# Turning attention probabilities in two 64-row halves of TensorE

## The chip, the core and the metric

The kernel runs on one core of a Trainium2 chip. The metric is the device time of one execution in microseconds (us), as the median of several runs. TensorE (PE in the rows) multiplies; its weight loads are shown as a row of their own, PEld. VectorE is DVE, ScalarE is ACT, GpSimd is POOL, SyncE is SP. Results of TensorE land in PSUM, which this kernel uses as eight banks of 512 float32 columns on 128 partitions.

## The reference

A decoder trunk of two layers on 512 positions of width 1024. Each layer runs a SwiGLU block, a mixer, a second SwiGLU block and a gated embedding. The mixer adds three kinds of heads. What matters here is the attention in it: 6 query heads in 2 key groups (sparse attention) and 4 differential heads.

```python
s_s = jnp.einsum('bqgrd,bgqkd->bgrqk', qblk, k_sel) * scale + bias
p_s = jax.nn.softmax(jnp.where((dist >= 0)[:, :, None], s_s, NEG), axis=-1)
o_s = jnp.einsum('bgrqk,bgqkd->bqgrd', p_s, v_sel)
...
s_w = jnp.einsum('bqgrd,bkgd->bgrqk', qblk, k_win) * scale + bias_w
p_w = jax.nn.softmax(jnp.where(valid_w, s_w, NEG), axis=-1)
o_w = jnp.einsum('bgrqk,bkgd->bqgrd', p_w, v_win)
...
a = p[:, :, 0] - lam * p[:, :, 1]
return jnp.einsum('bhqk,bkhd->bqhd', a, v)
```

## The kernel before

All matrices of weights stream through three slots: SP loads a chunk, ACT makes its high half (`weights_hi`, L983), DVE or POOL the low half (`weights_lo`, L1477 and L500), and TensorE does three products for each tile (L525 to L527). This part fills most of the time.

The attention works on ten **maps** for each layer, `u` = 0 to 9. Maps 0 to 5 are the sparse ones: `u // 2` is the head within a key group and `u % 2` says selected or window keys. Each holds both key groups, g = 0 and 1. Maps 6 to 9 are the differential heads. A map's probabilities lie in SBUF with the queries on the partitions, in four row blocks `i`, and for each block the key blocks `j` up to `i`: ten blocks of 128 x 128 for each g. To multiply them with the values, the keys must be on the partitions, so every block is turned: `transposes(u)` (L827) is a TensorE transpose with the block as the loaded weights and the identity as the moving operand. It writes PSUM, in three parts: part 0 has the 4 blocks of key block 0, part 1 the 3 of key block 1, part 2 the 3 of key blocks 2 and 3.

The turned blocks are copied to `probsT` in SBUF by ACT (`turned`, L1325) and by DVE (`evacuate`, L1897): ACT takes (g, part) = (0,0), (1,0), (0,2), DVE takes (0,1), (1,1), (1,2). Then `values(u)` (L847) multiplies.

The order of work on each engine is written out by hand. In step `u` TensorE does `transposes(u - 1)`, `scores(u + 1)` parts 0 and 1 (L815), `values(u - 1)`, `scores(u + 1)` part 2, and then, in the early steps, one input projection (24 large matmuls of L525 to L527), in steps 6 and later products of the output projection. ACT has in step `u` the exponentials of map u, `split` (the high half of the next weight chunk, L983, which waits until the projection just before the transposes is finished, since it needs its slot), and then its three copies. DVE has the logits of map u (L1883), the scaling of map u - 1 (L1917), the last logits, the scaling of the projection's result (L1613), in some steps a normalisation (L1633), and then its three copies.

PSUM banks for scores and turned blocks come from one list of five, in rotation: `take(content, 2)` gives the next bank and has TensorE wait until the engine that reads what it held five takes ago is done. The six takes of `transposes` are called T1 to T6 below, in the order (part 0, g 0), (part 0, g 1), (part 1, g 0) and so on; the scores that follow take S7 and S8 for part 0 together, and S9 and S10 for part 1. So T6 waits for the copy of T1, S7 for that of T2, S8 for T3, S9 for T4 and S10 for T5.

```python
SHARED = ((1, 0), (1, 1), (1, 2), (1, 3), (0, 3))
ACT_TURNS = {True: ((0, 0), (1, 0), (0, 2)), False: ((0, 0),)}
DVE_TURNS = {True: ((0, 1), (1, 1), (1, 2)), False: ((0, 1), (0, 2))}
```

Of the kernel before, what the change touches and what calls it, by code (L numbers as in the profile page):

```python
# [41 lines left out]
P = 128  # L42
# [147 lines left out]
def row0(i):  # L190

    return P * i * (i + 1) // 2


def col0(j):

    return P * (QT * j - j * (j - 1) // 2)
# [5 lines left out]
class Counts:  # L203
# [25 lines left out]
    def done(self, kind, *key, layer=None):  # L229

        if not self.known:
            return self.sem(kind), 1
        return self.sem(kind), self.known["seen"][(kind, self.layer if layer is None else layer, *key)]
# [13 lines left out]
def layers(nc, a, known):  # L247
# [3 lines left out]
    with ctx:  # L251
# [6 lines left out]
        def sb(name, shape, dt=F32):  # L258
            size = int(np.prod(shape[1:])) * 4
            t = nc.alloc_sbuf_tensor_at(name, shape, dt, offset=place["at"])  # L260
            place["at"] += (size + 63) // 64 * 64
            assert place["at"] <= 229344, (name, place["at"])
            return t
# [68 lines left out]
        place["at"] = hgrn0  # L332
        biasA = sb("biasA", [P, NSA_HEADS, SEQ])
        probs = [[sb(f"probs{u}{g}", [P, SCORES]) for g in range(NSA_KV)] for u in range(2)]
        probsT = [sb(f"probsT{g}", [P, SCORES]) for g in range(NSA_KV)]
        assert place["at"] <= gate0 + 4 * (2 * 6 * P + QT * 3 * P)
        place["at"] = hgrn0 + (P - hgrn0) % 2048
        mh, ml = sb("mixed_hi", [P, len(LATE), SEQ], F32R), sb("mixed_lo", [P, len(LATE), SEQ], F32R)
# [10 lines left out]
        def const_(name):  # L349
            at, n = CONST[name]  # L350
            return const[:, at:at + n]
# [46 lines left out]
        def bank_of(content):  # L398
            if not known:
                return main[0]  # L400
            which, n = known["bank"][(counts.layer, content)]
            return (main, side)[which][n % 4]

        def slot_of(name):

# [17 lines left out]
        with nc.Block() as block:  # L423
# [82 lines left out]
            def _(pe):  # L506
                turn, held = {0: 0, 1: 0, 2: 0}, {}

                def take(content, which=1, at=None):

                    if which == 2:
                        which, at = SHARED[turn[2] % len(SHARED)]
                        turn[2] += 1
                    elif at is None:
                        at = turn[which] % 4
                        turn[which] += 1
                    if (which, at) in held:
                        layer, old = held[which, at]
                        pe.wait_ge(*freed(old, layer=layer))
                    held[which, at] = (counts.layer, content)  # L520
                    counts.bank[(counts.layer, content)] = (which, at)
                    return (main, side)[which][at]
# [294 lines left out]

                def transposes(u):
                    for part, js in enumerate(((0,), (1,), (2, 3))):
                        for g in range(2 if u < NSA_HEADS else 1):  # L820
                            out = take(("t", u, g, part), 2)
                            pe.wait_ge(*done("probs_scaled", u, g, QT - 1))
                            to = 0
                            for j in js:
                                for i in range(j, QT):
                                    at = row0(i) + j * P
                                    mm = nc.tensor.transpose(out[:, to:to + P], probs[u % 2][g][:, at:at + P],  # L827
                                                             const_("ident"))
                                    to += P
                            mm.then_inc(*tick("turned_probs", u, g, part))  # L830

                outs = {}

                def values(u):
                    if u < NSA_HEADS:
                        r, b = u // 2, u % 2
                        if b == 0:
                            outs[r] = take(("nsa", r), 0, 2 * (r % 2))
                            pe.wait_ge(*freed(("cmp_turn", r)))
                            pe.wait_ge(*done("vc", 1))  # L840
                            nc.tensor.matmul(outs[r][:], vc[0:2 * CPAD, :], mixed[0:2 * CPAD, r, :],
                                             start=True, stop=False, skip_group_check=True)
                        for j in range(QT):
                            for g in range(NSA_KV):
                                rows = slice(HEAD * g, HEAD * g + HEAD)
                                pe.wait_ge(*freed(("t", u, g, min(j, 2))))
                                mm = nc.tensor.matmul(outs[r][rows, j * P:SEQ], vv[:, j, b, rows],  # L847
                                                      probsT[g][:, col0(j):col0(j + 1)], start=False,
                                                      stop=False, skip_group_check=True)
                    else:  # L850
                        d = u - NSA_HEADS
                        t = d // 2
                        if d % 2 == 0:
                            outs[3 + t] = take(("diff", t), 0, 2 * ((3 + t) % 2))
                        rows = slice(HEAD * (d % 2), HEAD * (d % 2) + HEAD)
                        for j in range(QT):
                            pe.wait_ge(*freed(("t", u, 0, min(j, 2))))
                            mm = nc.tensor.matmul(outs[3 + t][rows, j * P:SEQ], vv[:, j, 2 + t, rows],  # L858
                                                  dpT[:, col0(j):col0(j + 1)], start=(j == 0), stop=False,
                                                  skip_group_check=True)  # L860
                    mm.then_inc(*tick("values_used", u))
# [102 lines left out]
            def _(act):  # L964
# [352 lines left out]
                def turned(u, parts):  # L1317

                    for g, part in parts:
                        act.wait_ge(*done("turned_probs", u, g, part))  # L1320
                        a, b = ((0, 1), (1, 2), (2, 4))[part]
                        if u >= 1:
                            act.wait_ge(*done("values_used", u - 1))
                        to = probsT[g] if u < NSA_HEADS else dpT
                        nc.scalar.activation(to[:, col0(a):col0(b)],  # L1325
                                             bank_of(("t", u, g, part))[:, 0:col0(b) - col0(a)],
                                             ACT.Copy).then_inc(*tick("probsT_a", u, g, part,
                                                                      frees=("t", u, g, part)))

                def attention():  # L1330
# [133 lines left out]
            def _(dve):  # L1464
# [406 lines left out]
                def logits(u, rows):  # L1871

                    n = u - NSA_HEADS
                    dve.wait_ge(bias_in[n >= 0], 16 * (counts.layer + 1))
                    for i in rows:
                        part, at = max(i - 1, 0), P if i == 1 else 0
                        w = (i + 1) * P
                        for g in range(2):
                            bias = biasA[:, g * GROUP + u // 2, SEQ - w:SEQ] if n < 0 else biasB[:, n, SEQ - w:SEQ]
                            dve.wait_ge(*done("scores", u, g, max(i, 1)))  # L1880
                            if u >= 2:
                                dve.wait_ge(*done("turned_probs", u - 2, g if u - 2 < NSA_HEADS else 0, 2))
                            nc.vector.tensor_tensor_reduce(  # L1883
                                out=probs[u % 2][g][:, row0(i):row0(i + 1)],
                                in0=bank_of(("s", u, g, part))[:, at:at + w], in1=bias, scale=-1.0, scalar=3e38,
                                op0=ALU.add, op1=ALU.min, accum_out=sm("nm", 8 * (u % 2) + 4 * g + i)).then_inc(
                                    *tick("logits", u, g, i, frees=("s", u, g, part) if i else None))

                def evacuate(u, parts):

                    for g, part in parts:
                        dve.wait_ge(*done("turned_probs", u, g, part))
                        a, b = ((0, 1), (1, 2), (2, 4))[part]
                        if u >= 1:
                            dve.wait_ge(*done("values_used", u - 1))
                        to = probsT[g] if u < NSA_HEADS else dpT
                        nc.vector.tensor_copy(to[:, col0(a):col0(b)],  # L1897
                                              bank_of(("t", u, g, part))[:, 0:col0(b) - col0(a)]).then_inc(
                                                  *tick("probsT_v", u, g, part, frees=("t", u, g, part)))

                def scale(u):
# [314 lines left out]
```

## Time and profile before

| | us |
|---|---|
| median of 3 runs | 2266.33 |
| lowest, highest | 2265.96, 2266.48 |
| the profiled execution | 2266.42 |
| its span in the profile | 2264.6 |
| TensorE busy in it | 2225.9 |
| ACT busy, DVE busy | 895.4, 1196.2 |

The span is what the profile covers; 1.8 us of the profiled execution lie around it. Busy time counts a pipelined matmul until its end, so TensorE reads as busy also where it could take more. The granted clock of TensorE is 1.00 nearly throughout (2.4 GHz), with 0.50 (1.2 GHz) in a stretch that the rows below show.

### The profile page before, as it was taken

How to read it: one execution, taken by the hardware profiler on the slowest of the kernel's cores; microseconds unless marked ns; L12 is line 12 of the kernel's file. 1: busy time of each engine (PE TensorE's matmuls, PEld its weight loads, DVE VectorE, ACT ScalarE, POOL GpSimd, SP SyncE). 2: the span in 40 equal slices, each digit the busy share in tenths (PEclk: the TensorE clock that was granted, in tenths of full speed). 3: DMA queues.
4: the chain of work that ended last, by engine and by line, in shares of the span. 5: the costliest groups of instructions: out<-in, count | busy, mean ns of one | idle time of the engine just before them, and what ended most of it. 6: DMA issues, size and time to landing. Idle time of an engine off the chain costs nothing. (4 is left out here: it accounts for less than half of the span.)

```text
span 2264.6 us, 28786 instructions
## 1 busy us (share of the span) xinstructions
PE 2225.9 (98%) x11400; PEld 1762.8 (78%) x11400; DVE 1196.2 (53%) x1965; ACT 895.4 (40%) x1478; POOL 155.3 (7%) x155
## 2 busy tenths in 40 slices
PE   8999999999999999999999999999999999999999
PEld 6888888876657888888878888878766578888887
DVE  6444434577685444433664444346776854444336
ACT  5222223545574322222552322235566642232234
POOL 0000000033112000000000000000431110000000
PEclk9999999999999999999999999999999999999999
DMA  5433334322103332333223333343121123333332
GB/s 184 137 101 94 95 95 145 125 62 71 47 29 93 99 97 93 99 104 99 93 92 102 93 94 94 102 148 116 57 90 30 36 88 109 97 93 107 93 98 84
DMA packets 68991, 214.38 MB, mean 95 GB/s; under 512 B 8143, under 2 KB 15311, under 8 KB 68858
## 3 DMA queue, kind: packets, MB, share of 16 engines
q1 hardware_dynamic: 59344, 189.27, 27.4%
q10 hardware_dynamic: 9514, 23.27, 3.1%
q8 instruction: 91, 1.49, 0.3%
q14 instruction: 42, 0.34, 0.0%
HBM read 208.30 MB, written 5.40 MB: 94 GB/s over the span
## 5 line engine op out<-in xcount | busy, mean ns | idle before, releaser
L525 PE MATMUL main<-xh,wh 128*128 128x512 f32 x1896 | 755.3, 398 | 5.7 <-DVE wl L1477 2.8
L526 PE MATMUL main<-xl,wh 128*128 128x512 f32 x1896 | 739.6, 390 | 0.0
L527 PE MATMUL main<-xh,wl 128*128 128x512 f32 x1896 | 739.5, 390 | 0.0
L1477 DVE TENSOR_TENSOR wl<-raw,wh 128x1024 fp32r<-128x1024 f32 (+2 forms) x338 | 406.8, 1204 | 350.9 <-ACT wh L983 349.6
L983 ACT ACTIVATE wh<-raw 128x1024 fp32r<-128x1024 f32 (+3 forms) x372 | 378.0, 1017 | 494.7 <-PE main L527 467.4
L525 PEld LDWEIGHTS main<-xh,wh 128*128 128x128 f32 x1896 | 356.5, 188 | 107.1 <-issue 26.2
L526 PEld LDWEIGHTS main<-xl,wh 128*128 128x128 f32 x1896 | 356.6, 188 | 75.3 <-issue 4.3
L527 PEld LDWEIGHTS main<-xh,wl 128*128 128x128 f32 x1896 | 356.5, 188 | 75.2
L525 PE MATMUL main<-ffh,wh 128*128 128x512 f32 x704 | 273.9, 389 | 0.0
L526 PE MATMUL main<-ffl,wh 128*128 128x512 f32 x704 | 273.9, 389 | 0.0
L527 PE MATMUL main<-ffh,wl 128*128 128x512 f32 x704 | 273.9, 389 | 0.0
L1047 ACT ACTIVATE fg<-fg 128x512 f32<-128x512 f32 x88 | 55.6, 632 | 397.7 <-DVE fg L1569 397.7
L1569 DVE TENSOR_TENSOR fg<-main,rb 128x512 f32<-128x512 f32 x88 | 60.8, 691 | 248.4 <-PE main L527 216.3
L525 PEld LDWEIGHTS main<-ffh,wh 128*128 128x128 f32 x704 | 132.2, 188 | 27.5
L526 PEld LDWEIGHTS main<-ffl,wh 128*128 128x128 f32 x704 | 132.2, 188 | 27.4
L527 PEld LDWEIGHTS main<-ffh,wl 128*128 128x128 f32 x704 | 132.2, 188 | 27.4
L1582 DVE TENSOR_TENSOR fu<-main,rb 128x512 f32<-128x512 f32 x88 | 60.8, 691 | 147.2 <-PE main L527 147.2
L491 POOL TENSOR_TENSOR zv<-ev,hall 128x256 f32<-128x256 f32 x108 | 82.0, 782 | 258.4 <-ACT ev L1146 200.1
L1314 ACT ACTIVATE probs<-probs,small 128x128 f32<-128x128 f32 (+3 forms) x160 | 87.6, 552 | 7.7 <-DVE small L1883 7.7
L500 POOL TENSOR_TENSOR wl<-raw,wh 128x768 fp32r<-128x768 f32 (+1 forms) x34 | 69.3, 2042 | 257.5 <-ACT wh L983 257.5
L472 POOL MEMSET w2p<- 128x768 f32 x2 | 1.5, 740 | 1162.5 <-PE main L527 1162.5
L1736 DVE COPY_PREDICATED sdiag<-lmask,side 128x512 f32<-128x512 uint32 x84 | 57.0, 732 | 17.0 <-PE side L648 17.0
(246 smaller groups left out, 2059.5 us busy)
## 6 DMA issues: line engine op xcount, KB each, us to landing
raw<-in_ffn_gate SPq DMA_DIRECT2D x88, 512.0 KB, 3.6
raw<-in_ffn_up SPq DMA_DIRECT2D x88, 512.0 KB, 3.6
raw<-in_ffn_down SPq DMA_DIRECT2D x64, 448.0 KB, 3.3
raw<-in_w_in_t SPq DMA_DIRECT2D x40, 512.0 KB, 3.6
raw<-in_ffn_down SPq DMA_DIRECT2D x32, 512.0 KB, 3.5
raw<-in_wout SPq DMA_DIRECT2D x24, 384.0 KB, 3.2
w<-in_cmp_w ACTq DMA_DIRECT2D x16, 512.0 KB, 4.4
raw<-in_ple_gate SPq DMA_DIRECT2D x16, 512.0 KB, 3.4
```

Of the source, the lines that this page charges most:

```text
L491: nc.gpsimd.tensor_tensor(o.rearrange(cut, two=2, l=size)[:, :, which, :], e.rearrange(cut, two=2, l=size)[:, :, which, :], operand.rearra ...
L500: nc.gpsimd.tensor_tensor(wl[:, c % SLOTS, 0:n], raw[:, c % SLOTS, 0:n], wh[:, c % SLOTS, 0:n], ALU.subtract).then_inc(*tick("weights_lo_p ...
L525: nc.tensor.matmul(out, lh, rh, start=start, stop=False, **kw)
L526: nc.tensor.matmul(out, lh, rl, start=False, stop=False, **kw)
L527: return nc.tensor.matmul(out, ll, rh, start=False, stop=stop, **kw)
L983: nc.scalar.activation(wh[:, c % SLOTS, 0:n], raw[:, c % SLOTS, 0:n], ACT.Copy).then_inc(*tick("weights_hi", c, layer="all"))
L1047: nc.scalar.activation(fg[:, ft % 2, :], fg[:, ft % 2, :], ACT.Silu).then_inc(*tick("gate_silu", name, ft))
L1314: nc.scalar.activation(pr, pr, ACT.Exp, bias=sm("nm", k), scale=-1.0, accum_out=sm("sum", k)).then_inc(*tick("probs", u, g, i))
L1477: nc.vector.tensor_tensor(wl[:, c % SLOTS, 0:n], raw[:, c % SLOTS, 0:n], wh[:, c % SLOTS, 0:n], ALU.subtract).then_inc(*tick("weights_lo", ...
L1569: nc.vector.tensor_tensor(fg[:, ft % 2, :], bank_of((name + "_gate", ft))[:], rb[:], ALU.mult).then_inc(*tick("gate_scaled", name, ft, fre ...
L1582: nc.vector.tensor_tensor(fu[:, ft % 2, :], bank_of((name + "_up", ft))[:], rb[:], ALU.mult).then_inc(*tick("up_scaled", name, ft, frees=( ...
L1736: ins = V.copy_predicated(out, m, src)
```

## The change

For the six sparse maps each block of 128 queries x 128 keys is turned in two instructions in place of one: queries 0 to 63 as 64 x 128 weights on rows 0 to 63 of TensorE, queries 64 to 127 on rows 64 to 127, each with a 64 x 64 piece of the identity as moving operand. The two halves `h` write two different banks. A bank now holds one half of the queries of both key groups for a part, where it held all queries of one key group; its size is as before (8, 6 or 6 pieces of 64 columns). The copies read the same number of elements and write them in runs of 64 to `probsT`, which becomes one tile for both groups. The two banks of a part are taken together ahead of its first transpose. `values` waits for both banks of a part ahead of its first product of it, and the logits of map u wait for both halves of map u - 2. The differential maps are turned as before.

```diff
-        probsT = [sb(f"probsT{g}", [P, SCORES]) for g in range(NSA_KV)]
+        probsT = sb("probsT", [P, NSA_KV, SCORES])
...
+        def turned_places(u, h, bank, a, b):
+            if u >= NSA_HEADS:
+                return dpT[:, a:b], bank[:, 0:b - a]
+            to = probsT[:, :, a:b].rearrange("p g (n c) -> p g n c", c=P)[:, :, :, HEAD * h:HEAD * h + HEAD]
+            return to, bank[:, 0:b - a].rearrange("p (g n c) -> p g n c", g=NSA_KV, c=HEAD)
...
                 def transposes(u):
                     for part, js in enumerate(((0,), (1,), (2, 3))):
-                        for g in range(2 if u < NSA_HEADS else 1):
-                            out = take(("t", u, g, part), 2)
-                            pe.wait_ge(*done("probs_scaled", u, g, QT - 1))
+                        if u < NSA_HEADS:
+                            pair = [take(("t", u, h, part), 2) for h in range(2)]
                             to = 0
-                            for j in js:
-                                for i in range(j, QT):
-                                    at = row0(i) + j * P
-                                    mm = nc.tensor.transpose(out[:, to:to + P], probs[u % 2][g][:, at:at + P],
-                                                             const_("ident"))
-                                    to += P
-                            mm.then_inc(*tick("turned_probs", u, g, part))
+                            for g in range(NSA_KV):
+                                pe.wait_ge(*done("probs_scaled", u, g, QT - 1))
+                                for j in js:
+                                    for i in range(j, QT):
+                                        at = row0(i) + j * P
+                                        first = nc.tensor.transpose(pair[0][:, to:to + HEAD],
+                                                                    probs[u % 2][g][0:HEAD, at:at + P],
+                                                                    const_("ident")[0:HEAD, 0:HEAD])
+                                        second = nc.tensor.transpose(pair[1][:, to:to + HEAD],
+                                                                     probs[u % 2][g][HEAD:P, at:at + P],
+                                                                     const_("ident")[HEAD:P, HEAD:P])
+                                        to += HEAD
+                            first.then_inc(*tick("turned_probs", u, 0, part))
+                            second.then_inc(*tick("turned_probs", u, 1, part))
+                            continue
...
-                                pe.wait_ge(*freed(("t", u, g, min(j, 2))))
+                                if g == 0:
+                                    for h in range(2):
+                                        pe.wait_ge(*freed(("t", u, h, min(j, 2))))
                                 mm = nc.tensor.matmul(outs[r][rows, j * P:SEQ], vv[:, j, b, rows],
-                                                      probsT[g][:, col0(j):col0(j + 1)], start=False,
+                                                      probsT[:, g, col0(j):col0(j + 1)], start=False,
                                                       stop=False, skip_group_check=True)
...
                             if u >= 2:
-                                dve.wait_ge(*done("turned_probs", u - 2, g if u - 2 < NSA_HEADS else 0, 2))
+                                for h in range(2 if u - 2 < NSA_HEADS else 1):
+                                    dve.wait_ge(*done("turned_probs", u - 2, h, 2))
```

In the copies of ACT and DVE the target and the source come from `turned_places`.

## Rows read from the trace of the kernel before

**Rows 1.** The page: busy time, share of the span and instructions of TensorE.
```profile
PE 2225.9 (98%) x11400; PEld 1762.8 (78%) x11400; DVE 1196.2 (53%) x1965; ACT 895.4 (40%) x1478; POOL 155.3 (7%) x155
```

**Rows 2.** Line 827, the transposes: count, duration in ns min/median/max, first and last start, forms.
```profile
L827 PEld LDWEIGHTS side<-const,probs x259: 137/141/143, 573.4 to 1813.5; 128*128 128x128 f32 x130
L827 PE MATMUL side<-const,probs x259: 270/273/328, 573.6 to 1813.7; 128*128 128x128 f32 x130
L827 PE MATMUL main<-const,probs x61: 270/273/327, 574.5 to 1814.0; 128*128 128x128 f32 x61
```

**Rows 3.** Timeline of all TensorE weight loads at 575.45 us, merged where alike.
```profile
575.45 0.20 PEld L827 LDWEIGHTS side<-const,probs 128*128 128x128 f32 x2
```

**Rows 4.** Line 648, small matmuls of the HGRN scores, on quarters or halves of the array.
```profile
L648 PE MATMUL side<-zv x1344: 218/218/480, 454.8 to 1676.4; 64*64 64x64 f32 x180, 64*128 64x128 f32 x6, 64*128 64x256 f32 x6
```

**Rows 5.** Timeline of TensorE's matmuls, from a whole-array matmul to line 648.
```profile
454.51 0.39 PE L527 MATMUL main<-wh,xl 128*128 128x512 f32 x1
454.82 0.69 PE L648 MATMUL side<-zv 64*64 64x64 f32 x32
```

**Rows 6.** Timeline of TensorE: matmuls with 128-column weights and 64 moving columns.
```profile
532.85 2.34 PE L785 MATMUL side<-kc,q 128*128 128x64 f32 x20
```

**Rows 7.** Line 1713, a DVE operation whose output runs are 1 to 64 elements long.
```profile
L1713 DVE TENSOR_TENSOR ev<-hall x42: 410/418/622, 440.2 to 1665.6; 128x256 f32<-128x256 f32 x42
```

**Rows 8.** Line 827 in windows: length, PE busy (count), PEld busy (count), clock, DMA.
```profile
605.92:608.19 2.27, 2.27 (x20) 2.10 (x19) 1.00 0.01 4
```

**Rows 9.** Timelines of TensorE, its loads, ACT and DVE around the transposes of map 2.
```profile
608.19 0.93 PE L815 MATMUL side<-kk,q 64*128 64x128 f32 x8
...
608.19 0.52 PEld L815 LDWEIGHTS side<-kk,q 64*128 64x128 f32 x8 [0.17 <-ACT probsT L1325]
608.74 0.19 PEld L815 LDWEIGHTS main<-kk,q 64*128 64x128 f32 x1
...
606.17 0.84 ACT L983 ACTIVATE wh<-raw 128x768 fp32r<-128x768 f32 x1 [3.24 <-PE main L527]
606.92 1.54 ACT L1325 ACTIVATE probsT<-side 128x512 f32<-128x512 f32 x3
...
606.12 0.69 DVE L1613 TENSOR_TENSOR mixed<-main,rb 128x512 f32<-128x512 f32 x1 [3.40 <-PE main L527]
607.32 0.56 DVE L1897 COPY probsT<-side 128x384 f32<-128x384 f32 x1 [0.51 <-PE side L827]
```

**Rows 10.** The same of ACT and the loads for map 1, whose first transpose starts at 593.13.
```profile
594.36 0.58 ACT L1325 ACTIVATE probsT<-main 128x512 f32<-128x512 f32 x1
594.83 0.97 ACT L1325 ACTIVATE probsT<-side 128x512 f32<-128x512 f32 x2
...
595.47 0.96 PEld L815 LDWEIGHTS side<-kk,q 64*128 64x128 f32 x12 [0.18 <-ACT probsT L1325]
```

**Rows 11.** ACT for map 4, whose first transpose starts at 633.08.
```profile
633.72 1.09 ACT L1325 ACTIVATE probsT<-side 128x512 f32<-128x512 f32 x2 [1.75 <-PE side L827]
```

**Rows 12.** Timelines of TensorE's loads and of DVE for map 5.
```profile
645.18 0.64 PEld L827 LDWEIGHTS side<-const,probs 128*128 128x128 f32 x6 [0.30 <-DVE small L1883]
...
645.16 1.17 DVE L1897 COPY probsT<-side 128x384 f32<-128x384 f32 x2
...
646.32 0.95 PEld L815 LDWEIGHTS side<-dk,dqt 32*128 32x128 f32 x12 [0.17 <-issue]
```

**Rows 13.** Timeline of TensorE behind the transposes of map 0, layer 0.
```profile
578.51 0.34 PE L815 MATMUL side<-kk,q 64*128 64x128 f32 x1 [2.51 <-DVE probsT L1897]
```

**Rows 14.** Windows over map 0 of both layers: length, busy PE, PEld, DVE, ACT, POOL, clock.
```profile
573.60:578.51 4.91, 2.40 (x21) 2.11 (x20) 4.71 (x5) 3.81 (x8) 2.36 (x1) 1.00 0.06 15
578.51:586.48 7.97, 7.97 (x31) 3.34 (x31) 5.69 (x24) 3.06 (x12) 0.00 (x0) 0.57 0.17 49
1698.60:1703.52 4.92, 2.41 (x21) 2.12 (x20) 4.72 (x5) 3.81 (x8) 2.36 (x1) 1.00 0.05 11
1703.52:1708.15 4.63, 4.63 (x31) 2.39 (x31) 4.32 (x20) 3.06 (x12) 0.00 (x0) 1.00 0.35 84
```

More of the change, by code:

```diff
@@ new lines, in transposes @@
+                        out = take(("t", u, 0, part), 2)
+                        pe.wait_ge(*done("probs_scaled", u, 0, QT - 1))
+                        to = 0
+                        for j in js:
+                            for i in range(j, QT):
+                                at = row0(i) + j * P
+                                mm = nc.tensor.transpose(out[:, to:to + P], probs[u % 2][0][:, at:at + P],
+                                                         const_("ident"))
+                                to += P
@@ L832, in _ @@
+                        mm.then_inc(*tick("turned_probs", u, 0, part))
                 outs = {}
@@ L1323, in turned @@
                             act.wait_ge(*done("values_used", u - 1))
[L1324 to L1327, printed above, removed]
+                        to, came = turned_places(u, g, bank_of(("t", u, g, part)), col0(a), col0(b))
+                        nc.scalar.activation(to, came, ACT.Copy).then_inc(*tick("probsT_a", u, g, part,
                                                                       frees=("t", u, g, part)))
@@ L1895, in evacuate @@
                             dve.wait_ge(*done("values_used", u - 1))
-                        to = probsT[g] if u < NSA_HEADS else dpT
-                        nc.vector.tensor_copy(to[:, col0(a):col0(b)],
-                                              bank_of(("t", u, g, part))[:, 0:col0(b) - col0(a)]).then_inc(
+                        to, came = turned_places(u, g, bank_of(("t", u, g, part)), col0(a), col0(b))
+                        nc.vector.tensor_copy(to, came).then_inc(
                                                   *tick("probsT_v", u, g, part, frees=("t", u, g, part)))
```

## The prediction

> **What bounds the kernel.** I read the page first: TensorE is busy for 98% of the span [rows 1], so time changes only where TensorE's order of work gets shorter or waits differently. The change touches nothing but the attention of the sparse maps, so the second view is the line of the transposes. There are 320 of them (259 in the side banks, 61 in the main ones): 12 sparse maps x 20, and 8 differential ones x 10. Each matmul lasts 0.273 us and its load 0.141 [rows 2]. These are latencies. The pace is in the windows: in map 2 of layer 0, 19 loads fill 2.10 us, so (2.10 - 0.14) / 18 = 0.109 us a block, and 20 blocks hold TensorE for about 2.2 us, 26 us in the 12 maps [rows 8]. The third view is the timeline around them, for who waits. In map 2 the scores' first load starts at 608.19, just behind the last transpose; its release is put down to ACT's copy [rows 9]. Map 1 shows it too [rows 10]. In both, the transposes and the copies end at nearly the same moment, and this decides what faster transposes are worth.
>
> **Part 1, the pace of the transposes.** 240 transposes become 480, in 240 pairs. No row shows a transpose of half the rows, so I bound it. *Moving columns:* a matmul with 64 of them lasts 0.218 us [rows 4] and one with 128 lasts 0.273 [rows 2], so 64 cost 0.055 and 128 cost 0.109, just the pace of today. Moving is what sets it. *Weight load:* two loads of transposes, released together after a wait, take 0.20 us where one takes 0.14, so a 128-column load costs about 0.06 [rows 3, 2]. *Side by side:* L648 issues 32 matmuls of 64 x 64 on four quarters; all starts lie within 0.69 - 0.22 = 0.47 us, 0.059 us for a round of four, so pieces of the array do work side by side and the issue of instructions is no bound [rows 5]. From these three I take 0.058 us for a pair. It saves 20 x 0.051 = 1.0 us a map, 12.2 us in all, if nothing else ends later. The upper bound of a pair is 0.111, from the ordinary float32 matmuls with 128-column weights and 64 moving columns: (2.34 - 0.22) / 19 [rows 6]; beyond it stands 0.218, if two halves took turns at 0.109 each.
>
> Here the Trainium skill speaks against the change. "TensorE: Matmul & The Clock Gate", section "LDWEIGHTS (loading the stationary operand)", gives a load the time of its columns at 1.2 GHz, whatever the rows: an estimate by it is 128 / 1.2 = 107 ns for each half, so a pair would be no faster than a block is now. Rows 3 differ from it for transposes, Rows 6 agree for ordinary loads.
>
> **Part 2, the switch.** Today transposes follow whole-array matmuls and precede row-half scores. Between the last whole-array matmul and L648's first lie 0.31 us [rows 5]. With the change this step moves from behind the transposes to ahead of them. I count 0.1 us later for the first pair and the same back at the scores: zero. In map 5, where the scores use 32 rows, a switch of its own stays on both sides; 0.1 us at most in each layer.
>
> **Part 3, the banks.** T1 and T2 are complete together after eight pairs: 0.1 + 7 x 0.058 + 0.22 = 0.73 us behind the map's start; T3 and T4 at 0.1 + 13 x 0.058 + 0.22 = 1.07. Part 2 now takes T5 and T6 ahead of any of its blocks, so all of it waits for the copy of T1. That copy is bound by ACT, which first makes the weights' high half.
> - Map 2: that high half ends at 607.01 and the first copy starts at 606.92, 1.00 us behind the map's start [rows 9]. T1 is complete by then either way. With the 0.58 us of a copy [rows 10] it ends at 607.50; part 2 starts at 607.55 and its last pair at 607.9. S7 needs the copy of T2: it starts 0.47 us behind the first, takes 0.59 and is seen 0.05 us later [rows 10], so at 608.03, against 608.19 today. S10 needs T5, copied at about 608.15 to 608.65; its load comes 0.55 us behind S7's [rows 9], at 608.6, so this adds next to nothing. Gain 0.15 us, and the same in map 3, whose ACT has the same order.
> - Map 1: the high half is 0.2 us longer, the copy of T2 ends at 595.42 and the scores already start at 595.47 [rows 10]. Gain 0.
> - Map 4: ACT has no high half to make and starts its first copy at 633.72, 0.64 us behind the map's start, as soon as T1 is there [rows 11]. T1 now comes at 0.73 and the copy starts at 0.78; two copies in 1.09 us end at 634.95, S7 at 635.0. As the map has 2.27 us up to its scores like map 2 [rows 8], they start at 635.35 today. Gain 0.35 us.
> - Map 0: S7 and S8 wait 2.51 us for DVE's copy of T3 [rows 13], which a long DVE normalisation delays. Gain 0; this wait covers any pace up to about 0.2 us.
> - Map 5: today T3's blocks run ahead of the wait for the last logits, which ends at 645.18 [rows 12]. Now part 1 takes T3 and T4 together and all of it runs from 645.18: complete at 645.18 + 0.06 + 5 x 0.058 + 0.22 = 645.75. DVE's first copy moves from 645.16 to 645.78 and ends at 646.34; S8 at 646.39 against 646.32 [rows 12]. Loss 0.07 us.
>
> A layer gains 0.15 + 0.15 + 0.35 - 0.07 = 0.58 us, both 1.2 us. The rest of the 12.2 turns into waits for copies.
>
> **Part 4, at no cost.** The copies keep their sizes; their runs become 64 elements. A DVE operation with output runs from 1 to 64 elements takes 0.410 to 0.418 us in most of its 42 cases [rows 7], so I take zero; for ACT no row shows it, and 0.05 us a copy would cost up to 0.1 us in each of eight maps, 0.8 us. Behind the scores `values` queues on TensorE with its wait for both copies of a part; the 0.93 us of the first eight score matmuls alone [rows 9] cover the copies that come 0.1 to 0.2 us later. The extra wait of the logits is for transposes two maps back, and maps 1 and 2 start 13 us apart [rows 10, 8]. ACT's last exponentials of a map start up to 0.3 us later; DVE needs them only behind six logits of the next map. No DMA is moved.
>
> **Part 5, the clock.** In map 0 of layer 0 TensorE has 2.40 us of work and then waits; behind this the granted clock averages 0.57, so it is at 1.2 GHz for most of a stretch that takes 7.97 us. In layer 1 the same 2.41 us and the same wait leave it at 1.00, and the same work takes 4.63 [rows 14]. A fall costs 3.3 us. With the change the busy part of these 4.9 us shrinks from 2.4 to about 1.5 us, in two pieces, while the wait stays. Where the same stretch came out both ways, less work ahead of the wait makes the fall in layer 1 more likely than not; I count 6 in 10 if the pace is halved. In layer 0 I expect the fall to stay.
>
> **The sum.** The profiled execution had 2266.42 us, a span of 2264.6 and 1.8 around it. 2264.6 - 1.2 + 3.3 = 2266.7, with 1.8 around it 2268.5; the median of the runs shown stands 0.1 below that execution, which is within the rounding. I predict 2268.5.
>
> **The rivals.** 0.2% (4.5 us) is about what a measurement of this kernel tells from no change.
> - *Pace halved, clock as before in layer 1:* 2266.3 - 1.2 = 2265.1. For it: the clock of layer 1 in the rows. 0.25.
> - *Pace halved, second fall:* 2268.5. 0.40, of which 0.06 with one more fall, in map 5, where TensorE also waits: 2271.8.
> - *The weight load paces the pair at 0.111:* then the halves finish together at the old pace, T3 is complete at 0.1 + 13 x 0.111 + 0.22 = 1.76 in place of 1.4, S8 waits for DVE: 0.1 us lost in each of maps 1 to 4, 0.3 in map 5, 1.6 us in all: 2267.9, or 2271.2 with a second fall. For it Rows 6, against it Rows 3. 0.16, a third with a fall. The rule of the Trainium skill on loads, named above, leads to this case.
> - *The halves take turns, slower than before:* if transposes of two row halves cannot run side by side, a pair costs 0.218 and the ten maps beyond map 0 each lose 2.2 us: 2288. It decides above about 0.13 us a pair, where the waits for copies hide no more. Against it: scores on row halves start in pairs today, 8 loads in 0.52 us [rows 9]. 0.07.
> - *The gain shows in full, faster:* if the copies were no bound, ten maps would save 1.0 us each: 2256. Against it Rows 9 and 10. 0.06.
> - *The fall of layer 0 goes away:* 2266.3 - 1.2 - 3.3 = 2261.8. 0.06.
>
> Faster by over 0.2% (below 2261.8): 0.06 and half of the last case, 0.1. Slower (above 2270.9): 0.06 + 0.05 + 0.07, some 0.2. The rest, 0.7, is within 0.2%. The range goes from 2262.5, the halved pace with map gains twice as large, to 2272, which holds a third fall and the slow weight load with a second one; it leaves out about 0.2.
>
> **What would show it.** Pace: 40 transposes of L827's successor in pairs, starts 0.06 us apart, matmuls of 0.22 us. Banks: a gap of 0.5 to 0.9 us ahead of the last 12 transposes of maps 1 to 3, released by ACT's copy of T1; scores of map 1 at the same distance from the map's start (2.34), of map 2 at 2.1, of map 4 at 1.9. Clock: 0.5 behind map 0 of layer 1. Wrong would be: pairs 0.11 or 0.22 apart; ACT's copies starting earlier than 1.0 us in maps 1 to 3; copies longer than 0.59 us; or a clock that falls elsewhere.

## The result and the profile after

The changed kernel takes 2269.08 us, the median of 21 runs (2267.52 to 2274.31), against 2265.96 (2263.31 to 2266.87) for the kernel before in 21 runs beside it: 3.1 us slower. The ratio estimated from all runs is 1.002 [1.0014, 1.0027]; the two medians are 0.14% apart. The median is 0.6 us from the forecast. The profiled execution had 2269.02 us, with a span of 2267.2. The total is close; the places where the time went are not those forecast.

The page, for what [rows 1] showed before. TensorE has 240 instructions more, and the same share:
```profile
PE 2223.1 (98%) x11640; PEld 1756.2 (77%) x11640; DVE 1196.9 (53%) x1965; ACT 896.1 (40%) x1478; POOL 155.2 (7%) x155
```
The first halves by line, those in the side banks, for [rows 2]. A load lasts 138 ns where it had 141, a matmul 223 where the whole block had 273:
```profile
L836 PEld LDWEIGHTS side<-const,probs x180: 134/138/221, 572.9 to 1766.7; 64*128 64x128 f32 x180
L836 PE MATMUL side<-const,probs x180: 221/223/334, 572.9 to 1766.8; 64*128 64x64 f32 x180
```
The timeline of TensorE's matmuls through the transposes of map 2:
```profile
603.34 0.39 PE L535 MATMUL main<-xh,wl 128*128 128x512 f32 x1
603.66 0.27 PE L836 MATMUL side<-const,probs 64*128 64x64 f32 x1
...
603.84 0.22 PE L836 MATMUL side<-const,probs 64*128 64x64 f32 x1
603.90 0.22 PE L836 MATMUL side<-const,probs 64*128 64x64 f32 x1
...
605.25 0.24 PE L836 MATMUL side<-const,probs 64*128 64x64 f32 x1 [0.51 <-issue]
605.62 0.22 PE L839 MATMUL side<-const,probs 64*128 64x64 f32 x1
605.70 0.93 PE L823 MATMUL side<-kk,q 64*128 64x128 f32 x8
```
A pair every 0.06 us, a switch of 0.32 us from the last projection matmul, then a gap ahead of the last 12 transposes, and the scores 2.04 us behind the first transpose, where they came after 2.27 [rows 8, 9]. As the transposes themselves start 0.09 us later than before, the scores are 0.14 us nearer to the last projection matmul: 2.36 us for 2.50. ACT's timeline says what the gap waits for; its two copies from 604.58 are those that began at 606.92 in [rows 9]:
```profile
603.83 0.85 ACT L1010 ACTIVATE wh<-raw 128x768 fp32r<-128x768 f32 x1 [3.23 <-PE main L535]
604.58 1.07 ACT L1352 ACTIVATE probsT<-side 128x512 f32<-128x512 f32 x2
605.85 0.49 ACT L1352 ACTIVATE probsT<-side 128x384 f32<-128x384 f32 x1 [0.20 <-PE side L839]
```
Part 2's first load comes at 605.22, just behind the first of these copies (604.58 and the 0.58 of a copy [rows 10] make 605.16), and the scores at 605.70, behind the second (605.65).

Windows are the ledger. Each goes from the start of one last matmul ahead of a map's transposes to the next (a projection matmul; ahead of map 5 the second sum of squares, L560 before and L568 after); columns are length, busy PE, PEld, DVE, ACT and POOL, clock, DMA. Layer 0 of the kernel before, maps 0, 1, 2, 4 and 5, then map 5 of layer 1:
```profile
573.37:592.90 19.53, 17.02 (x79) 10.32 (x78) 11.71 (x32) 6.87 (x20) 2.36 (x1) 0.83 0.09 29
592.90:605.69 12.79, 12.79 (x78) 8.93 (x76) 8.39 (x30) 7.36 (x21) 2.37 (x1) 1.00 0.10 31
605.69:620.13 14.44, 14.44 (x82) 9.69 (x80) 8.36 (x30) 8.48 (x23) 1.82 (x1) 1.00 0.10 30
...
632.85:641.81 8.96, 8.96 (x58) 5.10 (x56) 7.95 (x25) 7.08 (x21) 0.00 (x0) 1.00 0.01 2
641.81:655.71 13.90, 11.65 (x68) 7.14 (x67) 12.75 (x40) 10.54 (x28) 1.82 (x1) 1.00 0.10 29
...
1763.47:1777.37 13.90, 11.64 (x68) 7.14 (x67) 12.75 (x40) 10.54 (x28) 1.82 (x1) 1.00 0.09 29
```
The same six of the kernel after, and map 0 of layer 1:
```profile
572.57:590.43 17.86, 14.71 (x99) 9.41 (x98) 11.78 (x32) 6.98 (x20) 2.35 (x1) 0.90 0.10 29
590.43:603.34 12.91, 12.19 (x97) 8.06 (x96) 8.41 (x30) 7.47 (x21) 2.36 (x1) 1.00 0.11 32
603.34:617.71 14.37, 13.86 (x101) 8.82 (x100) 8.47 (x30) 8.50 (x23) 1.82 (x1) 1.00 0.09 29
...
630.45:639.23 8.78, 8.42 (x77) 4.22 (x76) 7.91 (x25) 6.98 (x21) 0.00 (x0) 1.00 0.01 3
639.23:655.07 15.84, 13.80 (x88) 8.15 (x87) 13.90 (x44) 10.75 (x29) 1.82 (x1) 0.78 0.08 25
1697.74:1713.91 16.17, 13.02 (x99) 8.57 (x98) 11.72 (x32) 6.98 (x20) 2.35 (x1) 1.00 0.10 32
1762.68:1779.96 17.28, 15.21 (x89) 8.71 (x87) 14.22 (x45) 10.76 (x29) 1.82 (x1) 0.70 0.07 24
```
Map 0 of layer 0 is 1.67 us shorter, map 1 0.12 longer, map 2 0.07 and map 4 0.18 shorter, map 5 1.94 longer in layer 0 and 3.38 in layer 1. Maps 1 to 4 of layer 1 repeat layer 0 within 0.03, and its map 0 is unmoved. Beside this the first window begins 0.8 us earlier, a shift that is there at 30 us already (29.98 against 29.20 us for the first matmul that sums squares), ahead of all changed work; in the profiles of the runs below this window begins anywhere from 571.61 to 573.27, so I take it for scatter between executions. The clock is in the last columns: not one fall more behind map 0 of layer 1 (1.00), but one in each map 5. Their extent, after:
```profile
578.00:581.40 3.40, 3.40 (x14) 1.87 (x11) 2.71 (x15) 1.89 (x9) 0.00 (x0) 0.50 0.28 100
...
642.90:649.70 6.80, 6.76 (x44) 3.77 (x44) 5.18 (x16) 3.62 (x9) 0.94 (x1) 0.50 0.20 58
...
1765.80:1776.00 10.20, 9.73 (x54) 5.29 (x56) 8.18 (x28) 4.92 (x12) 1.50 (x1) 0.50 0.12 39
```
and before, where there was one alone:
```profile
579.50:586.30 6.80, 6.80 (x22) 2.38 (x18) 4.90 (x22) 3.06 (x12) 0.00 (x0) 0.50 0.07 24
```
So two things were open: what the change is worth without the clock, and what brings the clock down in map 5.

### The profile page after: what moved, and what is told of

It is laid out like the page before. It is cut to its first block and busy times, and to the rows that moved or that the text cites. A ratio compares the mean times of both kernels' runs of the same rounds, so it can differ in the third digit from the quotient of the medians.

```text
span 2267.2 us, 29302 instructions
## 1 busy us (share of the span) xinstructions
PE 2223.1 (98%) x11640; PEld 1756.2 (77%) x11640; DVE 1196.9 (53%) x1965; ACT 896.1 (40%) x1478; POOL 155.2 (7%) x155
```

## The experiments

Each had 11 runs (the fourth 10) beside the kernel before. e1 to e4 ran together, then f1 to f4, then g1 and g2; the medians of the kernel before were 2266.06, 2265.52 and 2266.19 beside these three sets, so a difference of medians between two sets is good to some 0.5 us. In all but e1 and e4 the falls are taken out by filler matmuls, so that what is left can be compared in windows of the profiled executions:

| layer 0, us | map 0 | map 1 | map 2 | map 3 | map 4 | map 5 |
|---|---|---|---|---|---|---|
| before, filled (e2) | 16.20 | 12.78 | 14.45 | 12.72 | 8.96 | 13.96 |
| after, filled (e3) | 16.18 | 12.91 | 14.37 | 12.70 | 8.78 | 14.32 |
| before, filled, late weights (f1) | 15.80 | 12.72 | 14.45 | 12.72 | 8.96 | 13.91 |
| after, filled, late weights (f2) | 15.77 | 12.57 | 14.22 | 12.61 | 8.78 | 14.29 |
| bank order alone, filled (f3) | 16.23 | 13.14 | 14.63 | 12.93 | 10.99 | 12.97 |
| after, filled, map 5 whole (f4) | 16.18 | 12.91 | 14.37 | 12.70 | 8.77 | 13.99 |

These are windows cut as above; in f3 the border between maps 4 and 5 lies elsewhere, so their sum (23.96) is what compares.

**e1_map5_whole.** The changed kernel with map 5 turned as before, in whole blocks, one bank at a time (WHOLE is (5,)).
```
-                        if u < NSA_HEADS:
+                        if u < NSA_HEADS and u not in WHOLE:
```


> The changed kernel with map 5 alone turned as before (whole blocks, one bank for each key group, banks taken one by one), maps 0 to 4 in halves. Theory A (the loss of the change lies in map 5: its blocks now wait together for the last logits, and the clock falls there in both layers): without it the falls behind map 5 go away, 1.9 us in layer 0 and 3.3 in layer 1 come back, so some 2264 us against 2269.1 for the change and 2266 before; granted clock 1.00 behind map 5 in both layers. Rival B (the loss is spread over all maps, by copies and banks that come free later): one sixth of it goes, 2268 to 2269.

Measured: 2267.97 us (2265.06 to 2270.84), 1.001 [1.0001, 1.0019]. The windows of its profiled execution (2270.84 us):
```profile
580.00:586.40 6.40, 6.40 (x22) 2.14 (x19) 4.36 (x18) 2.83 (x12) 0.00 (x0) 0.50 0.01 3
1702.00:1713.00 11.00, 9.56 (x32) 4.52 (x34) 7.23 (x26) 3.97 (x16) 0.28 (x1) 0.53 0.12 36
641.00:650.00 9.00, 7.80 (x52) 4.36 (x50) 7.85 (x21) 7.61 (x17) 1.82 (x1) 1.00 0.14 44
1766.00:1782.00 16.00, 13.65 (x79) 7.76 (x75) 14.78 (x49) 12.41 (x36) 1.82 (x1) 1.00 0.09 26
```
Both falls in map 5 are gone (1.00), as theory A said. But a long one now stands behind map 0 of layer 1 (0.53), where I had first forecast it and the change did not have it, though map 0's instructions are the same in both. The runs lie in groups at 2265.1 to 2265.6 (four) and 2270.3 to 2270.8 (five), with two between, and the profiled execution is of the upper one. So the median, which is the one that rival B gave, speaks neither for B nor against A: it depends on where the clock fell in each execution. In this profile, undoing one map's halves moved a fall; it did not take it away.

**e2_fill_before** and **e3_fill_after.** Both kernels with work for TensorE in its waits. In e2 ten float32 matmuls of constants follow the transposes of map 0, into a main bank that is free; e3 has these and twice three in the waits of map 5.
```
+                def fill(n):
+                    layer, old = held[0, 1]
+                    pe.wait_ge(*freed(old, layer=layer))
+                    for _ in range(n):
+                        nc.tensor.matmul(main[1][:, 0:P], const_("ones"), const_("ones"), start=True, stop=True)
...
                             transposes(u - 1)
+                        if u == 1:
+                            fill(10)
```


> The kernel before, with ten matmuls of 128 x 128 x 128 of constants added behind the transposes of map 0 in both layers, where TensorE waits 2.5 us for DVE's copy; they are 2.1 us of work into a bank that nobody reads. Theory A (the fall of the clock there comes from TensorE standing idle): no fall, 3.3 us less, 2262.7. Rival C (the clock falls for another reason than idle time, or filler does not hold it): 2266, or more by what of the filler is not covered.

> The changed kernel with the same filler behind map 0, and three such matmuls in each of the two waits of map 5 (for the second key group's probabilities, and for the banks of part 1). Theory A: no falls in the attention; the change without its falls is worth what its shorter stretches say, between 0 and 1.2 us less than the kernel before without its fall: 2261.5 to 2262.7. Rival B (the loss is waiting, not clock): 2267 to 2269.

Measured: e2 2262.91 us (2261.89 to 2263.36), 0.9986 [0.9977, 0.9995]; e3 2263.13 (2262.22 to 2263.92), 0.9987 [0.9978, 0.9995]. The filler in the timeline of e2:
```profile
574.40 2.40 PE L823 MATMUL main<-const 128*128 128x128 f32 x20
```
and its window:
```profile
571.93:588.13 16.20, 15.90 (x99) 11.65 (x98) 11.64 (x32) 6.87 (x20) 2.37 (x1) 1.00 0.10 33
```
Maps 0 and 5 of e3:
```profile
572.48:588.66 16.18, 15.45 (x120) 10.88 (x118) 11.64 (x32) 6.99 (x20) 2.36 (x1) 1.00 0.10 33
...
637.41:651.73 14.32, 12.35 (x100) 8.10 (x99) 12.70 (x41) 10.75 (x29) 1.82 (x1) 1.00 0.10 29
```
With 2.40 us of work in the wait, map 0 takes 16.20 us in place of 19.53, and the clock is 1.00 throughout: the fall costs 3.3 us, just as [rows 14] gave it. One of the 33 runs of the kernel before beside f1 to f4 says the same without any filler: its mean granted clock was 1.000, and it took 2263.25 us. In the changed kernel the fillers are worth 6.0 us. Without any fall the change costs 0.2 us (2263.13 - 2262.91) in place of the gain of 1.2 that I summed; e3 lies outside the 2261.5 to 2262.7 expected of it. By the table a layer loses 0.13 in map 1 and 0.36 in map 5 and gains 0.08 in map 2, 0.02 each in maps 0 and 3 and 0.18 in map 4. Of the loss in map 5 part is the filler itself. The last logit ends, and the loads behind the filler start:
```profile
640.75 0.08 DVE L1922 DVE_READ_ACCUMULATOR2_ANT small<- 128x1 f32 x1
...
640.22 0.74 PEld L831 LDWEIGHTS main<-const 128*128 128x128 f32 x6
641.09 0.14 PEld L847 LDWEIGHTS side<-const,probs 64*128 64x128 f32 x1
```
In the kernel before the loads come 0.05 us behind that logit (645.13, 645.18 in [rows 12]), here 0.26. So some 0.2 us of the 0.36 is filler, and 0.15 the change; that estimate takes the change without falls to -0.2 us over both layers by the medians, and to 0 by the windows: nothing, in any case.

**e4_group_only.** The kernel before, its whole blocks in the bank order of the change: both banks of a part are taken and filled by turns, once both groups are there.
```
-                            mm.then_inc(*tick("turned_probs", u, g, part))
...
+                        for n, (j, i) in enumerate(at_):
+                            for g in groups:
+                                at = row0(i) + j * P
+                                mm = nc.tensor.transpose(pair[g][:, n * P:n * P + P], probs[u % 2][g][:, at:at + P],
+                                                         const_("ident"))
```


> The kernel before, whole blocks of 128 x 128, but the two banks of a part are taken together and both key groups of a part finish together, as in the change; the pace of a block stays 0.109 us. It shows the order of banks alone. My sum for the old pace in this order was 0.1 us lost in each of maps 1 to 4 and 0.3 in map 5, 1.6 us in all: 2267.6, and 2270 or more if the clock falls behind map 5 too. If the order of banks costs nothing: 2266.

Measured: 2271.52 us (2270.71 to 2274.0), 1.0027 [1.0017, 1.0036]. The clock falls five times, 3.4 us each. Two of them, and the first transpose of map 5 with the wait ahead of it:
```profile
576.00:580.50 4.50, 3.75 (x14) 2.37 (x14) 3.54 (x15) 2.08 (x9) 0.00 (x0) 0.62 0.29 87
641.00:645.50 4.50, 4.07 (x22) 3.93 (x24) 2.53 (x8) 2.09 (x5) 1.81 (x1) 0.62 0.12 36
...
641.43 0.45 PE L828 MATMUL main<-const,probs 128*128 128x128 f32 x1 [1.73 <-DVE probs L1918]
```
Falls come in map 5 with whole blocks too, so the halved pace is not needed for them. That the waits alone bring them is not shown by it: this kernel waits for both key groups ahead of its first block, once and for 1.73 us, and its clock is down at 641.2 already, inside that wait; the changed kernel begins with the blocks of the first group and has shorter waits. Order and clock are mixed here too, which f3 takes apart.

**f3_group_fill.** e4's order with the fillers of e3.

> The kernel before in the change's order of banks (pairs of banks, both groups finishing together) with whole blocks at the old pace, and filler in maps 0 and 5, so that no fall of the clock blurs it. By my sum this order costs 1.6 us: 2264.5 against 2262.9 for the kernel before with filler; the changed kernel with filler stands at 2263.1, so the pace would be worth 1.4. If the order is free: 2262.9, and the pace is then worth nothing.

Measured: 2266.15 us (2265.47 to 2268.47), 1.0007 [0.9998, 1.0016], no fall in the profiled execution. Five of its 11 runs lie 1.6 to 2.3 us above this median, which no profile explains. Against e2 the order costs 3.2 us, twice the 1.6 expected, and against e3 the halved pace gives back 3.0; the windows of both layers give 3.6 and 3.2. Every map from 1 on pays, by the table 0.36, 0.18, 0.21 and, in maps 4 and 5 together, 1.04. Some of the last is filler that e2 does not have: in map 5 the last logit ends at 642.24 and part 1's loads start at 642.57, 0.33 us behind it, for 0.05 in the kernel before. Without these 0.28 us a layer the order costs about 3.1 us by the windows. The pace is worth as much, as e3's filler overruns too, by 0.21 us a layer. ACT in its map 2:
```profile
602.67 0.84 ACT L997 ACTIVATE wh<-raw 128x768 fp32r<-128x768 f32 x1 [3.25 <-PE main L527]
603.42 1.07 ACT L1339 ACTIVATE probsT<-side 128x512 f32<-128x512 f32 x2
604.88 0.49 ACT L1339 ACTIVATE probsT<-side 128x384 f32<-128x384 f32 x1 [0.39 <-PE side L839]
```
Counted from the last projection matmul (602.19) the first two copies stand where they do in the kernel after, as they begin behind the high half; the third is late, since its bank is filled last.

**f4_map5_whole_fill.** e3 with map 5 in whole blocks.

> The changed kernel with map 5 turned as before and filler behind map 0 and in map 5's wait for the second key group. What map 5 in halves costs apart from the clock: by my sum 0.07 us a layer plus a switch; by the trace of the change the wait of part 1 for both banks costs more, 0.3 to 0.5 us a layer. I expect 2262.3 against 2263.1 with halves; 2263.0 if my sum was right.

Measured: 2262.51 us (2261.61 to 2263.03), 0.9986 [0.9977, 0.9994], 0.6 us under e3 and 0.4 under e2, near the 2262.3 expected. Map 5 takes 13.99 us for e3's 14.32; about 0.2 of these 0.33 us are e3's second filler there, which this kernel leaves out. The other maps are those of e3.

**f1_before_late_split** and **f2_after_late_split.** e2 and e3, with ACT's high half of the next weights behind its copies in the maps.
```
-                        if u in TILE_AT:
+                        if u == 0:
                             split(CHUNK[(TILE_AT[u],)] + AHEAD)
...
                         if u:
                             turned(u - 1, ACT_TURNS[u - 1 < NSA_HEADS])
+                        if u and u in TILE_AT:
+                            split(CHUNK[(TILE_AT[u],)] + AHEAD)
```


> The kernel before with the filler behind map 0 (the base without a fall of the clock, 2262.9 us), and in steps 1 to 4 ACT makes the high half of the next weight chunk behind its three copies, not ahead of them, so the copies no longer wait for it. The transposes at the old pace set S7 then, not the copies: transposes end 2.2 us behind the start of the map, scores already start 0.1 us later. I expect 0 to 0.5 us less than that base.

> The changed kernel with filler in maps 0 and 5 (2263.1 us) and the same move on ACT. If the halved pace is worth nothing because T6, S7 and S10 wait for ACT's copies, copies that start 0.3 to 0.4 us earlier let it show: 0.3 us in each of maps 1 to 3 of both layers, 1.5 to 2 us less than its base. If something else holds it (DVE's copies, the switch of the array), the same as its base.

Measured: f1 2261.74 us (2260.53 to 2262.27), 0.9982 [0.9974, 0.9991]; f2 2260.92 (2260.16 to 2261.5), 0.9979 [0.9971, 0.9988]. Timelines of f2, map 2, whose first transpose loads at 601.72:
```profile
602.47 1.09 ACT L1365 ACTIVATE probsT<-side 128x512 f32<-128x512 f32 x2 [3.83 <-PE side L850]
...
603.13 0.14 PEld L847 LDWEIGHTS side<-const,probs 64*128 64x128 f32 x1 [0.47 <-issue]
...
603.60 0.52 PEld L823 LDWEIGHTS side<-kk,q 64*128 64x128 f32 x8
```
The copies start 0.75 us behind the first transpose in place of 0.92, and the scores 1.88 in place of 2.04. The move is worth 2.2 us with halves (f2 - e3) and 1.2 with whole blocks (f1 - e2); in maps 1 to 3 the halves gain 0.34, 0.15 and 0.09 by it, the whole blocks 0.06, 0 and 0. So the faster blocks were ready, and ACT was not.

The rest is map 0, where both gain 0.4 us, and that was in neither expectation; f1 was to gain 0.5 us at most. There the high half is also what GpSimd waits for to make the low half. DVE and GpSimd in map 0 of the kernel before, then DVE in f1:
```profile
575.07 2.83 DVE L1633 SCALAR_TENSOR_TENSOR dk<-mixed,cols,rn 128x512 f32<-128x512 f32 x1
...
574.99 2.36 POOL L500 TENSOR_TENSOR wl<-raw,wh 128x1024 fp32r<-128x1024 f32 x1 [6.83 <-ACT wh L983]
...
573.97 0.74 DVE L1644 SCALAR_TENSOR_TENSOR dk<-mixed,cols,rn 128x512 f32<-128x512 f32 x1
```
The normalisation that makes TensorE wait in map 0 is long where it starts beside GpSimd's work: 2.83 us there, and 0.74 in f1 and f2, where GpSimd starts later (576.07 in f1), in both layers each time. In f1 DVE's copy of T3 ends at 575.18, 2.91 us behind the last projection matmul where e2 has 5.03, but the scores start only at 577.01, behind the filler (574.68 and its 2.40 us). The wait of 2.5 us is gone, and now the filler is what holds TensorE, for about 1.8 us a layer by these rows (577.01 less 575.18). The late high half without the filler in map 0 was not run; f1, f2 and g2 may leave up to 3.6 us there.

**g1_part1_twice.** e3, where the six pairs of part 1 are issued twice into the same places in maps 0 to 4.
```
-                            for g in range(NSA_KV):
+                            for g in list(range(NSA_KV)) * (2 if part == 1 and u < 5 else 1):
```


> The changed kernel with filler in maps 0 and 5 (2263.1 us), and every pair of part 1 issued twice in maps 0 to 4: six pairs more a map, at 0.06 us 3.5 us of TensorE in all, into the same bank with the same result. If the pace is covered by the wait ahead of part 2 for ACT's first copy, the time stays at 2263.1 (within 0.4). If the transposes are on the path, up to 3.5 us more.

Measured: 2263.32 us (2262.94 to 2264.35), 0.9988 [0.998, 0.9997], 0.2 us over e3 for 120 transposes more. Its map 2, whose first load is at 602.10:
```profile
603.67 0.13 PEld L849 LDWEIGHTS side<-const,probs 64*128 64x128 f32 x1 [0.25 <-issue]
...
604.27 0.55 PEld L823 LDWEIGHTS side<-kk,q 64*128 64x128 f32 x8
```
Twelve transposes more in the map cut the gap in the loads from 0.62 to 0.25 us, and part 2 begins 1.57 us behind the start, against 1.56 without them (603.66 to 605.22): up to there they lie wholly beside ACT's work. The scores come later, 2.17 us behind the start for 2.04, behind DVE's copy of T3, which ends at 604.16; of this 0.05 us is left in the length of the map (14.42 us for e3's 14.37).

**g2_best.** Halves in maps 0 to 4, whole blocks in map 5, the fillers and the late high half together.

> Halves in maps 0 to 4, map 5 as before, filler behind map 0 and in map 5's wait, ACT's high half behind its copies in steps 1 to 4. The steps of the parts add: 2260.9 for the changed kernel with filler and the move, less the 0.6 to 0.7 us that map 5 in halves cost, 2260.2. That is 1.5 less than the kernel before with filler and the same move (2261.7). If the gains do not add: 2260.9.

Measured: 2260.46 us (2259.55 to 2261.31), 0.9976 [0.9967, 0.9985], clock 1.000: 5.5 us under the kernel before (2265.96) and 8.6 under the kernel after. Expected were 2260.2, or 2260.9 if the gains do not add; they nearly add. Most of it is not the change: of the 5.5 us the filler alone gave 3.1 (e2) and the late high half 1.2 more (f1, 2261.74). The halves are worth the last 1.3, once ACT is out of their way and map 5 is left whole; the windows of the two layers give 1.3 as well.

## Why the prediction was right, and where it was not

- **Pace (part 1): right.** Pairs start 0.06 us apart, with matmuls of 0.22: 20 pairs hold TensorE for 1.2 us where 20 blocks held it for 2.2. Neither the weight load nor turns between the halves set the pace. The Trainium skill ("TensorE: Matmul & The Clock Gate", section "LDWEIGHTS (loading the stationary operand)") would have every load take an estimated 107 ns (128 / 1.2) for its 128 columns, whatever the rows; here each row half gets a new load of 128 columns every 60 ns, so by the trace the rule does not hold for these transposes.
- **Switch (part 2): right.** It starts the transposes 0.32 us behind the last projection matmul in place of 0.23, and the scores follow 0.08 us behind the last pair (605.62, 605.70). In map 4 it shows at the scores: they start at 632.72, 0.13 us behind the end of ACT's second copy, when part 2 and the switch behind it are through.
- **Banks (part 3): right in kind, one wait mis-sized.** Part 2 waits for ACT's first copy as described, and S7 comes at 2.25, 2.04, 2.04 and 1.95 us behind the first transpose in maps 1 to 4. The forecast of 2.34, 2.1, 2.1 and 1.9 counts from where the transposes started before, 0.09 us earlier; from there it is 2.34, 2.13, 2.13 and 2.04. The step that failed is "this adds next to nothing", said of S10, which waits for T5. The scores' loads of map 1, after, which ran in one piece before [rows 10], and the second piece of map 3:
```profile
593.00 0.52 PEld L823 LDWEIGHTS side<-kk,q 64*128 64x128 f32 x8
593.75 0.33 PEld L823 LDWEIGHTS side<-kk,q 64*128 64x128 f32 x4 [0.23 <-DVE probsT L1923]
...
620.83 0.33 PEld L823 LDWEIGHTS side<-kk,q 64*128 64x128 f32 x4 [0.20 <-issue]
```
  T5 and T6 are filled last of all, side by side, and ACT's copy of T5 ends at 593.64, DVE's of T6 at 593.75. By the rotation S10 needs ACT's. The row names DVE's, which ends at the same moment, but in map 3 the loads go on at 620.83, 0.12 us behind ACT's copy and ahead of the end of DVE's (620.89). From the last projection matmul S7 comes as late in map 1 as before (2.57 us), so the wait of 0.23 us is a loss of 0.12 to 0.13. In maps 2 and 3 S7 is 0.14 to 0.15 us earlier, just my 0.15; the waits of 0.23 and 0.20 leave 0.07 to 0.09 of it in map 2 and nothing beyond 0.02 in map 3. Map 4 keeps 0.18 for my 0.35: its S7 is 0.24 us earlier, and it waits 0.16. Map 5 loses about 0.15, not 0.07. A layer thus gains nothing instead of 0.58 us. The table and e3 - e2 (+0.2 us) show it. "The rest turns into waits for copies" held: g1 shows the room in those waits, f2 that an earlier ACT opens part of it, and f3 where the pace did earn its keep: about 3 us, which pay for the about 3 that the bank order costs.
- **Copies (part 4): right.** In map 2 ACT's two take 1.07 us, as against 1.09 in [rows 11], and DVE's 0.55 to 0.56 as in [rows 9], with runs of 64 elements.
- **Clock (part 5): right in sign, wrong in place.** I put a second fall behind map 0 of layer 1 and gave map 5 a chance of 0.06. Instead the fall of map 0 in layer 0 halved (-1.67 us; e3 has 16.18 without one), map 0 of layer 1 kept its clock, and each map 5 lost it: 15.84 and 17.28 us against e3's 14.32, so 1.5 and 3.0 us, or 0.2 more each without that map's filler. The step that failed is looking only at the longest wait. In map 5 the loads have two waits of 0.8 and 0.9 us with bursts of transposes between them. TensorE's loads in it, after:
```profile
641.48 0.14 PEld L836 LDWEIGHTS main<-const,probs 64*128 64x128 f32 x1 [0.77 <-DVE probs L1942]
...
642.72 0.14 PEld L836 LDWEIGHTS side<-const,probs 64*128 64x128 f32 x1 [0.91 <-DVE small L1909]
```
  In the kernel before, part of T3's blocks ran between them, and [rows 12] show 0.30 us at the second; after, all of part 1 waits there. The clock is down from 642.9. In the 4.10 us from the first sum of squares (638.70) to 642.80 TensorE is busy for 2.10 us. In the kernel before, in the 4.10 us from the same instruction on (641.27), it is busy for 3.00 us and the clock stays up. That this difference brings the fall is argued, not shown; that filler in these waits prevents it is shown (e3).
- **The sum.** The parts: start-up scatter -0.8, map 0 of layer 0 -1.7, maps 1 to 4 -0.1 to -0.2 a layer, map 5 +1.9 and +3.4: together +2.6 us, the distance of the two profiled executions. I had -1.2 and +3.3 for +2.1. That the total agrees is luck in good part: the map gains were about 1.2 us too good, the clock lost 2.8 us net (-1.7 + 1.5 + 3.0) where I had 3.3, and -0.8 us was not the change's.

**What stays open.** e2, e3 and f4 show that the falls, and not the transposes, carry the loss, and that work in the waits removes it. In which wait the clock falls is not explained: e1 has a fall behind map 0 of layer 1 with instructions that keep the clock in the kernel after, and the kernel before, which has a fall in its profile, had none in one run of 33. No run filled a wait with transposes in place of matmuls. Of the changed kernel's 21 runs 13 lie at 2267.5 to 2270.1 and 8 at 2271.3 to 2274.3; I take a further fall for the cause of the second group: the mean granted clock is 0.993 in six of its eight runs, where it is 0.995 or 0.996 in all 13. But the one profiled execution is of the first group.

## What to carry to other kernels

When a block gets faster, ask first who empties what it fills: here ACT's and DVE's copies ended as late as before, and filling two banks side by side delayed the last one, so twice the pace bought back only the cost of its own bank order. Where TensorE waits near a stage at full load, price the clock for every wait that grows, short ones included, and try a few matmuls of constants in the longest: ten of them were worth 3.1 us here, more than the halves of the blocks in any order. But ask first what makes the wait. Here it was a DVE operation that took 2.83 us beside GpSimd's work and 0.74 without it; moving one ACT operation removed it, and the filler then outlasted the wait. Fit the filler again whenever the work around it moves.

## What the runs showed of the hardware

- Float32 transposes of 64 rows on the two row halves start as pairs 0.06 us apart, half the 0.109 us of a whole block [rows 8], at 0.22 us a matmul and 0.138 a load.
- Copies from a bank into two places with runs of 64 elements take what contiguous ones take: 0.58 us for 512 elements on ACT, 0.55 for 384 on DVE.
- A DVE operation of 128 x 512 float32 with two SBUF inputs (L1633) that starts beside GpSimd's low half of the weights takes 2.83 us, in both layers of the kernel before; with GpSimd idle it takes 0.74 (f1, f2).
- The granted clock stood at 1.2 GHz for 3.4, 6.8 or 10.2 us. A stretch of 6.8 us that TensorE fills costs 3.3 us (map 0, before), one of 10.2 us with waits in it 3.0 (map 5, after).
- Without a change in the work before them, the same instructions kept or lost the clock from one kernel to the next (map 0 of layer 1 in the kernel after and in e1), and the runs of the kernels with falls spread over 3.3 to 6.8 us, where those of the filled ones stay within 1.8 (f3 alone within 3.0).
